# Two column chunks of the down projections as one pair of 1 MB units, with seven block products in eight of them

## What is computed

```
h = x + 1/2 * RMSNorm(SwiGLU_1(RMSNorm(x)))       # (silu(u @ w_gate) * (u @ w_up)) @ w_down
u = RMSNorm(h);  z = u @ w_in                      # RG-LRU heads and short convolutions
h = h + RMSNorm(concat(A, B) @ w_out)
h = h + 1/2 * RMSNorm(SwiGLU_2(RMSNorm(h)))
```

## Time and profile before

| | us |
|---|---|
| median of 3 runs (1771.12 to 1771.35) | 1771.31 |
| the profiled execution | 1769.51 |
| its span | 1767.4 |

### The profile page before, as it was taken

One profiled execution on the slowest core, in us unless ns is written; L12 is line 12 of the kernel. 1 busy time (PEld: TensorE's weight loads), 2 busy tenths in 40 slices (PEclk: granted clock), 3 DMA queues, 4 the chain that ended last, 5 costly groups with the idle time before them and its releaser, 6 DMA issues.

```text
span 1767.4 us, 22273 instructions
## 1 busy us (share of the span) xinstructions
PE 1746.9 (99%) x7832; PEld 1438.5 (81%) x7832; DVE 1288.1 (73%) x1176; ACT 934.3 (53%) x957; POOL 141.1 (8%) x129
## 2 busy tenths in 40 slices
PE   8999999999999999999999999999999999999998
PEld 6878888888888888788888878888888888888886
DVE  6889898989864444655686568989898898854444
ACT  7655555555554334556654446555555555544442
POOL 5100000000000000100000007000000000000000
PEclk9999999999999999999999999999999999999999
DMA  7777777777585556665565557777878777566554
GB/s 238 231 222 217 227 229 226 224 218 227 173 292 196 179 178 220 193 206 171 164 199 169 203 166 249 232 221 217 239 217 232 217 227 224 200 222 210 201 185 148
DMA packets 159954, 371.62 MB, mean 210 GB/s; under 512 B 11916, under 2 KB 14100, under 8 KB 158996
## 3 DMA queue, kind: packets, MB, share of 16 engines
q1 hardware_dynamic: 148628, 350.33, 60.7%
q0 software_dynamic: 11232, 20.45, 7.5%
q10 hardware_dynamic: 32, 0.01, 0.0%
HBM read 366.55 MB, written 4.19 MB: 210 GB/s over the span
## 4 chain that ended last, share of the span: by engine, by line
PE 85%; DMA 7%; DVE 5%; issue 1%; ACT 1%; POOL 0%; DVEq 0%; SPq 0%; ACTq 0%
PE ps L1272 15%; PE ps L1274 15%; PE ps L1273 15%; PE ps L1374 13%; PE ps L1376 13%; PE ps L1375 13%; DMA u_raw<-in_ffn_w_up 4%; DVE w_lo L880 1%; DVE u_lo L991 1%; DMA u_raw<-in_ffn_w_gate 1%; PE ps L1369 1%; DMA raw<-in_w_in 1%; ACT w_hi L580 1%; PE ps L1509 0%; PE ps L1308 0%
## 5 line engine op out<-in xcount | busy, mean ns | idle before, releaser
L880 DVE TENSOR_TENSOR w_lo<-raw,w_hi 128x1024 fp32r<-128x1024 f32 x316 | 394.7, 1254 | 348.3 <-ACT w_hi L580 344.8
L580 ACT CAST w_hi<-raw 128x1024 fp32r<-128x1024 f32 x320 | 335.0, 1053 | 388.7 <-PE ps L1274 342.6
L677 ACT CAST u_hi<-u_raw 128x2048 fp32r<-128x2048 f32 x160 | 305.7, 1911 | 154.8 <-DMA u_raw<-in_ffn_w_up 76.3
L991 DVE TENSOR_TENSOR u_lo<-u_raw,u_hi 128x2048 fp32r<-128x2048 f32 x160 | 364.2, 2286 | 8.7 <-ACT u_hi L677 4.6
L1272 PE MATMUL ps<-w_hi,hT_hi 128*128 128x512 f32 x832 | 324.3, 390 | 0.8 <-DVE w_lo L880 0.8
L1274 PE MATMUL ps<-w_hi,hT_lo 128*128 128x512 f32 x832 | 323.8, 389 | 0.0
L1273 PE MATMUL ps<-w_lo,hT_hi 128*128 128x512 f32 x832 | 323.7, 389 | 0.0
L1374 PE MATMUL ps<-u_hi,xT_hi 128*128 128x512 f32 x648 | 252.5, 390 | 0.4 <-DVE act_g L1028 0.4
L1376 PE MATMUL ps<-u_hi,xT_lo 128*128 128x512 f32 x648 | 252.3, 389 | 0.0
L1375 PE MATMUL ps<-u_lo,xT_hi 128*128 128x512 f32 x648 | 252.1, 389 | 0.0
L684 ACT CAST t_hi<-tsum 128x1536 fp32r<-128x1536 f32 x78 | 115.7, 1483 | 145.0 <-DVE tsum L1004 91.3
(11 more groups left out here) (143 smaller groups left out, 1982.7 us busy)
## 6 DMA issues: line engine op xcount, KB each, us to landing
raw<-in_ffn_w_down SPq DMA_DIRECT2D x176, 512.0 KB, 4.3
u_raw<-in_ffn_w_gate SPq DMA_DIRECT2D x42, 1024.0 KB, 5.1
u_raw<-in_ffn_w_up SPq DMA_DIRECT2D x40, 1024.0 KB, 5.1
raw<-in_w_in SPq DMA_DIRECT2D x80, 512.0 KB, 3.9
u_raw<-in_ffn_w_up SPq DMA_DIRECT2D x80, 256.0 KB, 4.0
u_raw<-in_ffn_w_up SPq DMA_DIRECT2D x40, 512.0 KB, 3.7
u_raw<-in_ffn_w_gate SPq DMA_DIRECT2D x76, 256.0 KB, 4.0
u_raw<-in_ffn_w_gate SPq DMA_DIRECT2D x38, 512.0 KB, 3.7
```

The lines of the kernel that those rows point to most:

```text
L580: sc.copy(w_hi[:, s], raw[:, s]).then_inc(hi_ready, 1)
L677: sc.copy(unit(u_hi, p), unit(u_raw, p)).then_inc(unit_hi, 1)
L880: ve.tensor_tensor(w_lo[:, s], raw[:, s], w_hi[:, s].bitcast(f32), ALU.subtract).then_inc(lo_ready, 1)
L991: ve.tensor_tensor(unit(u_lo, p), unit(u_raw, p), unit(u_hi, p).bitcast(f32), ALU.subtract).then_inc(unit_lo, 1)
```

## The change

Of the 22 groups of rows of a down projection's chunks 2 and 3, the first 36 tiles of rows are taken as 18 units (`DU`) of 256 rows by 1024 columns. The eight odd ones from 1 to 15 (`DS`) are done with seven block products, the others with eight. Products N1, N5, N6 and N7 gather in banks 0 to 3, which are free because the outputs of chunks 0 and 1, multiplied by the gain, now go to SBUF (`kept`). N2, N4, N3, N8 in banks 4 to 7 receive everything else, also the last four groups of each chunk, as single groups (`down_last`); combinations of N1, N5, N6, N7 (`down_rest`) are added to them at the end (`add_rest`). The forms for all eight units are made from the hidden activations during chunk 1, by VectorE and ScalarE. High and low parts of the units lie over the rings, the residual and the transposed input; sums of weights lie over the gain, whose second half is loaded again, and the residual is loaded after the units. Chunk 1 goes group by group to its end. Its core, with the slots:

```diff
+    rest = [(j + 2) % SLOTS for j in range(GF)]
...
-    for name, n, pattern in (("up1", 2, four), ("down1", NC, odd), ("in", 5 * JC, four),
-                             ("out", NC, four), ("up2", 2, four), ("down2", NC, odd)):
+    for name, n, pattern in (("up1", 2, four), ("down1", 1, odd + rest + four), ("in", 5 * JC, four),
+                             ("out", NC, four), ("up2", 2, four), ("down2", 1, odd + rest + four)):
...
+        LO_REST = LO.replace("post:0", "rest:0 post:0").replace("split:1", "rest:1 split:1")
```

SyncE, in `ffn`:

```diff
-                    if j == 12:
-                        sync.dma_start(resid[:], keep if f else x_v).then_inc(resid_back, 16)
-                with sync.Fori(0, NC - 1) as it:
-                    load_chunk(Place(down + GF, it, GF), w_down, it + 1, range(GF))
+                pl = Place(down + GF)
+                load_chunk(pl, w_down, 1, range(GF))
+                for p in range(DU):
+                    if p % 2 and p < 4:
+                        sync.wait_ge(lo_ready, pl.count(GF - 4 + p))
+                    elif p == 2:
+                        sync.wait_ge(d_form, 8 * (f + 1))
+                    elif p >= 4:
+                        sync.wait_ge(d_used, d_count(f, p - 4))
+                    sync.dma_start(d_raw[d_place(p)].rearrange("p (k n) c -> p k (n c)", k=GK),
+                                   w_down[:, GK * p:GK * p + GK, 2 * W:4 * W]).then_inc(d_full[p % 4], 16)
+                last = Place(down + 2 * GF)
+                for j in range(2 * SLOTS):
+                    if j == 2:
+                        sync.wait_ge(d_used, d_count(f, DS[-1]))
...
+                    if j == SLOTS - 1:
+                        load_gain((f1_post, f2_post)[f], 2 * W)
+                        for t in range(TOK):
+                            sync.dma_start(resid[:, t], keep[:, t] if f else x_v[:, t]).then_inc(resid_back, 16)
```

ScalarE, in `ffn`:

```diff
-                summed_chunks(down, GF, GP)
+                for j in range(GF):
+                    if j == GP:
+                        act.wait_ge(w_used, Place(down).count(GF - 1))
+                        for t in range(TOK):
+                            bank_square(0, t, kept(0))
+                    split(Place(down + GF), j)
+                    if 3 <= j < 11 and j % 2:
+                        form_hi_of_down(f, (j - 3) // 2)
+                down_hi(f, 0)
+                down_hi(f, 1)
+                act.wait_ge(w_used, Place(down + GF).count(GF - 1))
+                for t in range(TOK):
+                    bank_square(1, t, kept(1))
+                for p in DS:
+                    down_hi(f, p + 1)
+                    down_sums_hi(f, p)
+                    down_hi(f, p + 2)
+                    if p == DS[-1]:
+                        act.wait_ge(n1_done, f + 1)
+                        sc.copy(rest_of[:, 0, 0], bank(N1)).then_inc(n1_out, 1)
+                last = Place(down + 2 * GF)
+                for j in range(2 * SLOTS):
+                    split(last, j)
+                for t in range(TOK):
+                    act.wait_ge(rest_added, 2 * TOK * f + t + 1)
+                    bank_square(2, t)
+
+            def form_hi_of_down(f, n):
+                act.wait_ge(d_form, 8 * f + 2 * n + 2)
+                sc.copy(xg[:, :, n, 0], xg32[:, :, n, 1]).then_inc(d_form_hi, 1)
+
+            def down_hi(f, p):
+                n = d_place(p)
+                act.wait_ge(d_full[p % 4], d_loaded(f, p))
+                if p < 4:
+                    old = Place(starts[f"down{f + 1}"] + GF)
+                    act.wait_ge(w_used, old.count(GF - 3 + p // 2 * 2))
+                elif p == DU - 1:
+                    act.wait_ge(d_used, d_count(f, DS[-1]))
+                if p in DS:
+                    act.wait_ge(d_pair, ds_count(f, p))
+                sc.copy(d_hi[n][:], d_raw[n][:]).then_inc(d_hi_done, 1)
+
+            def down_sums_hi(f, p):
+                act.wait_ge(d_sums, 2 * ds_count(f, p))
+                if p > DS[0]:
+                    act.wait_ge(d_used, d_count(f, p - 2))
+                sc.copy(dsum_hi[:], dsum[:]).then_inc(dsum_hi_done, 1)
```

VectorE, in `ffn`. `down_form` is a sum or difference of 128 x 2048 tiles for an even number (activations, high and low together, for all eight units) and an addition of its two halves, 128 x 1024, for an odd one; each waits for the one before. `down_sums` waits for the seven-product unit before to be used:

```diff
-                summed_chunks(2 * f, down, GF, GP + 2)
+                for j in range(GF):
+                    if j == GP + 2:
+                        for t in range(TOK):
+                            gain_bank(2 * f, 0, t)
+                    split(Place(down + GF), j)
+                    if 2 <= j < 10:
+                        down_form(f, j - 2)
+                    elif 12 <= j < 16:
+                        down_form_lo(f, j - 12)
+                down_lo(f, 0)
+                down_pair(f, DS[0])
+                for t in range(TOK):
+                    gain_bank(2 * f, 1, t)
+                for p in DS:
+                    down_sums(f, p)
+                    down_lo(f, p)
+                    down_sums_lo(f, p)
+                    down_lo(f, p + 1)
+                    if p < DS[-1]:
+                        down_pair(f, p + 2)
+                down_rest(f)
+                down_lo(f, DU - 1)
+                last = Place(down + 2 * GF)
+                for j in range(2 * SLOTS):
+                    split(last, j)
+                for t in range(TOK):
+                    add_rest(f, t, 2)
+                for t in range(TOK):
+                    gain_bank(2 * f, 2, t)
...
+            def down_pair(f, p):
+                b = d_raw[d_place(p)]
+                dve.wait_ge(d_full[p % 4], d_loaded(f, p))
+                ve.tensor_tensor(b[:, B12], b[:, B11], b[:, B12], ALU.add).then_inc(d_pair, 1)
...
             ffn(1)
+            add_rest(1, 0, NC - 1)
             for t in range(TOK):
                 post_norm(2, t)
                 gain_bank(2, NC - 1, t)
                 for c in range(NC):
                     update(2, NC * t + c, t, c)
+                    if t == 0 and c == 0:
+                        add_rest(1, 1, NC - 1)
```

`down_rest` is four instructions on 512 columns, the first of which waits for the copy of N1. `add_rest(f, t, c)` adds one 128 x 512 part to a bank; for c = 3 it waits for the end of that token's matmuls, and `last_square` now waits for it. TensorE:

```diff
-                summed_chunks(down, GF, None if f else 1)
+                pl = Place(down + GF)
+                for j in range(GF):
+                    group(pl, j, hT_hi, hT_lo, j, GF, (bank(2), bank(3)))
+                for p in range(DU):
+                    down_unit(f, p)
+                down_last(f, Place(down + 2 * GF), None if f else 1)
```

More of the change, by code:

```diff
@@ L113, in hybrid_block_kernel @@
     assert FC == 2 * PAIRS + 1 and SEVEN == (0, 2, 4, 6) and NS % 2 == 0
+    DU = GF - SLOTS
+    DS = tuple(range(1, DU - 2, 2))
+    ND = len(DS)
+    N1, N5, N6, N7, N2, N4, N3, N8 = range(8)
+    S1, S2, S4, D1 = range(4)
+    assert GF == 22 and NC == 4 and ND == 8 and DS[-1] == DU - 3
     def lin(q, a, b):
@@ L589, in last_square @@
             def last_square(d, t):
-                if t == 0:
-                    act.wait_ge(tok0_done, NC * (d + 1))
+                if d != 1:
+                    act.wait_ge(rest_added, 2 * TOK * (d // 2) + TOK + t + 1)
+                elif t == 0:
+                    act.wait_ge(tok0_done, 2 + NC)
                 else:
-                    act.wait_ge(w_used, starts[("in", "up2", "end")[d]])
+                    act.wait_ge(w_used, starts["up2"])
                 bank_square(NC - 1, t)
@@ L923, in hand_over @@
                 pl = Place(starts[PHASE[r]])
-                for what, n in order(LO_FIRST if r == 0 else LO):
+                for what, n in order((LO_FIRST, LO_REST, LO)[r]):
                     if what == "split":
@@ L932, in hand_over @@
                         post_norm(r - 1, n)
+                    elif what == "rest":
+                        add_rest(0, n, NC - 1)
                     elif what == "bank":
@@ new lines, in down_sums_lo, with down_rest @@
+            def down_sums_lo(f, p):
+                dve.wait_ge(dsum_hi_done, ds_count(f, p))
+                ve.tensor_tensor(dsum_lo[:], dsum[:], dsum_hi[:].bitcast(f32), ALU.subtract).then_inc(dsum_lo_done, 1)
+            def down_rest(f):
+                n11, n12, n21, n22 = (rest_of[:, t, n] for t in range(TOK) for n in range(2))
+                dve.wait_ge(n1_out, f + 1)
+                dve.wait_ge(n6_done, f + 1)
+                ve.tensor_tensor(n12, bank(N6), n11, ALU.add).then_inc(rest_ready, 1)
+                dve.wait_ge(n7_done, f + 1)
+                dve.wait_ge(rest_ready, 4 * f + 1)
+                ve.tensor_tensor(n21, n12, bank(N7), ALU.subtract).then_inc(rest_ready, 1)
+                ve.tensor_tensor(n12, bank(N5), n12, ALU.subtract).then_inc(rest_ready, 1)
+                dve.wait_ge(rest_ready, 4 * f + 2)
+                ve.tensor_tensor(n22, bank(N5), n21, ALU.subtract).then_inc(rest_ready, 1)
@@ new lines, in add_rest @@
+            def add_rest(f, t, c):
+                pl = Place(starts[f"down{f + 1}"] + 2 * GF)
+                dve.wait_ge(rest_ready, 4 * (f + 1))
+                if c == 2:
+                    dve.wait_ge(w_used, pl.count(SLOTS - 1))
+                elif t == 0:
+                    dve.wait_ge(tok0_done, (2 + NC) * f + 2)
+                else:
```

(63 more changed lines are left out.)

99 lines of the change are left out of this document (88 added, 11 removed).

## The result

The changed kernel takes 1799.14 us in the median (4 runs, 1797.38 to 1802.21) against 1771.21 (4 runs): ratio 1.0159, 95% interval 1.0147 to 1.0172. It is slower by 27.9 us, where 20.1 were forecast. The median lies 0.9 us under the upper end of the range of 8 in 10 (1780 to 1800), and two of the four runs lie above it. The profiled execution took 1800.1 us with a span of 1798.3.

The account below looks back on a forecast made before the run. TensorE was taken as the bound, at 0.2267 us per matmul. Stalls of 13.6 against 5.44 saved per projection, twice 16.3, plus 1.9 and 1.95 make 20.1 on 1771.3: 1791.4 us, 8 in 10 from 1780 to 1800.

Parts of the forecast that it names:

- The saving: Down projections: 24 matmuls fewer in each, 48 in all, at 0.2267 us each, 10.9 us.
- The turned ring: Start of chunk 1: beginning in slot 2, which comes free later than slot 0, makes TensorE start 1.3 us late.
- The forms in chunk 1: Chunk 1: ScalarE's casts wait for forms with high parts queued behind; TensorE starts group 10 9.1 us late, ring's 1.3 included.
- The recurrence's steps of 3.36 and 4.48 us: Chunk 1: low part to low part, even to odd group 3.36, odd to even 4.48; together 7.84 against TensorE's 5.44.
- that the forms would be absorbed: Rival, chunk 1: the ring absorbs the forms, only the joints cost, +4.4 us, 1775.7; chance 0.11.
- Unit 1 and unit 17: Units' first and last joints: low parts queued behind other VectorE work, 2.4 us lost at unit 1, 2.1 at unit 17.
- The middle units: Steady units: VectorE 8.9 and ScalarE 5.3 of TensorE's 10.2 us per pair, loads in time; costed at nothing.
- The end: After the last matmul: three updates of token 0 queue behind the second addition, reduction 1.95 us later.
- The hand-over: First hand-over: later transposes and the second addition delay the reduction and the update TensorE waits on, 1.9 us.
- its factor 1.26: Chunk 1's forms: longest case for strided reads, from 864 against 686 ns, 12.8 us; the plain durations were taken instead.
- The clock: Rival: the clock falls in the stalls, +3.2 us for the 3.0 us stall alone, +19 for all six per projection; chance 0.07.
- the milder clock case: Clock rival with a fall in the 3.0 us stall alone: +3.2 us, 1794.6; the rival's chance is 0.07.

Follow-up runs that it names:

- all_seven: Changed kernel with all edits together, the forms spread over every other group of chunk 1: 1764.25 us, ratio to the kernel before 0.9963.
- ring_order: Changed kernel with chunk 1 beginning in slot 0 again, with chunk 0's slot pattern: 1796.8 us in a single run.
- casts_late: Changed kernel with the forms' four ScalarE casts moved from behind high parts 3, 5, 7, 9 to behind 10 to 13: 1784.44 us, ratio to before 1.0069.
- pool_after: Changed kernel with GpSimd's first low part in the first hand-over also waiting for the update of block 2: 1793.13 us in a single run.
- first_seven: Changed kernel with unit 1's block sum ahead of unit 0's low part, its weight sums and low part ahead of chunk 1's gains: 1790.47 us, single run.
- unit17_first: Changed kernel with VectorE doing unit 17's low part ahead of the four instructions of the rest: 1792.77 us in a single run.
- before_again: The kernel before, unchanged, traced a second time on the chip of the experiments: 1770.9 us, span 1768.7.

## Why the prediction was right, and where it fell short

- **The saving** was sized right: 48 matmuls of 0.2267 us. It shows in full once the waits are gone: in all_seven chunks 2 and 3, to the last matmul, are 5.5 and 5.4 us shorter than before.
- **The turned ring**: 1.3 us forecast, 1.23 and 1.26 measured, and ring_order took it away.
- **The forms in chunk 1**: 9.1 with the ring, 8.86 measured (1.23 + 7.63). The forms took the plain durations that the forecast had chosen, 2.28 and 1.22 us. The waits start to start less 0.23, before groups 6 to 10 of projection 1, are 1.5, 0.5, 2.7, 0.5 and 1.5; each costs a further 0.11, because the matmul after the first one comes 0.34 us behind it and not 0.23. The recurrence's steps of 3.36 and 4.48 us are 3.35 and 4.41 in the trace (556.35 - 553.00, 560.76 - 556.35). The 0.08 us of overlap that the forecast subtracts does not come out of the row it names (0.59 long, 0.58 apart); the rows above bear it out (1.22 long, 1.13 apart). Its rival, that the forms would be absorbed, is what casts_late shows when the wait is taken away, and only then.
- **Unit 1 and unit 17**: forecast 2.4 and 2.1, together 4.5. Without a clock fall 18 units last 97.57 us (pool_after, projection 1) against 92.55 without the waits, 5.0; first_seven takes off 2.65, unit17_first 2.28.
- **The middle units** at nothing: right.
- **The end**: 1.95 forecast, 2.0 measured; moving the addition gave back 1.1.
- **The hand-over**: 1.9 forecast, 4.87 measured. The step "the second addition delays the reduction" was right (3.0 us after the last matmul in place of 1.3, 1.7 later), and with GpSimd's part out of the way the stretch is 1.8 us longer than before (pool_after). What failed is the step that left the update's duration at 0.75 us: its operand had moved to SBUF, and it met GpSimd (2.86 us). That made TensorE's wait 2.1 us longer, and after this wait of 3.4 us the clock fell as well; together 3.1 us. The Trainium skill, "SBUF — State Buffer", section "Who interferes with whom", says that a VectorE instruction with two SBUF inputs and a GpSimd instruction that reads SBUF exclude each other for a whole instruction; both traces agree: the update that meets GpSimd's instruction ends 0.5 us after it, in the changed kernel (742.06 and 741.52) and in pool_after (739.44 and 738.90). The sign stood in the old trace. The 864 ns from which the forecast took its factor 1.26 are a mean of ordinary instructions of 0.68 us and of three that ran beside GpSimd, up to 1.77 us long; the forecast used the mean for the forms, and did not ask the question of the update:

```profile
1089.79 1.77 DVE L972 TENSOR_TENSOR xf<-xf,xf 128x512 fp32r<-128x512 f32 x1
...
1092.63 0.68 DVE L972 TENSOR_TENSOR xf<-xf,xf 128x512 fp32r<-128x512 f32 x1
```

```profile
1088.66 2.36 POOL L537 TENSOR_TENSOR xf<-x,xf 128x512 f32<-128x512 f32 x1
```

- **The clock**: it was a rival at 0.07, and it happened. After the wait for unit 1 in the changed kernel:

```profile
616.72 0.39 PE L1608 MATMUL ps<-d_hi,hT_all 128*128 128x512 f32 x1
619.58 0.50 PE L1606 MATMUL ps<-d_hi,hT_all 128*128 128x512 f32 x1 [2.48 <-DVE d_lo L1295]
619.92 0.39 PE L1607 MATMUL ps<-d_lo,hT_all 128*128 128x512 f32 x1
...
620.93 0.63 PE L1608 MATMUL ps<-d_hi,hT_all 128*128 128x512 f32 x1
621.36 0.63 PE L1606 MATMUL ps<-d_hi,xg 128*128 128x512 f32 x1
621.79 0.63 PE L1607 MATMUL ps<-d_lo,xg 128*128 128x512 f32 x1
```

Matmuls come 0.43 us apart, the lower of the two levels (1.2 in place of 2.4 GHz), here 1.1 us after TensorE has gone on working: the granted clock is 1.00 from 619.6 to 620.7 and 0.50 from 620.8 to 624.1. Other falls came between 0.5 us before TensorE went on and 1.5 us after. The mean granted clock of the first projection's units is 0.97, in a window where it was 1.00 in all_seven. The same 18 units last 97.57, 99.16 and 100.81 us with no, one and two such falls: 1.6 us each, the price given in the prediction. The changed kernel's trace has five: one hidden in chunk 1, where the next low part was late anyway, three in the units, one at the hand-over. Whether the clock falls at a wait of the same length differs from one place to another and from trace to trace. Counted over the seven traces with such waits, it fell at 13 of the 24 waits of about 2.9 us (start to start), at 6 of the 12 of 2.4, at all five of 3.4, and at none of 1.8 or less. What failed in the prediction is the step "no stall of that kind stands in the old trace" as a reason against: the old trace had none because it had no wait of that length.
- **What the forecast was short by**: 7.8 us between the medians. Three clock falls in the units are 4.8, and the hand-over 3.0 (4.87 - 1.9), its own fall included. The mechanism of the main loss, in chunk 1, was right and its size too; that the median stayed inside the range is partly luck, because the range had room for only the milder clock case and none for the hand-over's meeting, and a fall more or less moves a run by 1.6 us.

The sum by its terms: per projection 1.25 + 7.64 + 5.0 - 5.44 = 8.45 (8.1 forecast), twice 16.9; clock in the units 4.8; hand-over 4.9; end 2.0; together 28.6, against 27.9 between the medians. The 30.9 us between the two spans hold 2.35 more in the stretches ahead of the projections, of which before_again shows 1.4 (1.16 and 0.27) without the change.
